# Folding the two key blocks of a windowed attention into one square of scores

## The reference

```
dist = arange(w)[:, None] + w - arange(2 * w)[None, :]
valid = (dist >= 0) & (dist < w) & (key_abs >= 0)
s = where(valid, s - slopes * dist, -inf)
m = maximum(max(s, axis=-1), sink)
p = exp(s - m)
p = p / (sum(p, axis=-1) + exp(sink - m))
o = einsum('bnhgqk,bnkhd->bnqhgd', p, vb)
return (o * silu(z)) @ w_out
```

## Time and profile before

| | |
|---|---|
| median of 3 runs | 1959.88 us (1953.9 to 1959.93) |
| profiled execution, its own time | 1960.14 us |
| its span | 1958.4 us |
| PE busy | 1878.6 us (96% of the span) |
| DVE busy | 1139.6 us (58%) |
| ACT busy | 717.4 us (37%) |
| layer 1's four groups | from about 1314 us to 1750 us of the span |

### The profile page before, as it was taken

The page is one execution under the profiler, slowest core; times in us unless marked ns, Lnnn a source line. Parts: engine busy times, 40 slices in busy tenths (PEclk is TensorE's granted clock), DMA queues, the critical chain, the costliest instruction groups (busy, mean ns, idle before and its releaser), DMA issues.

```text
span 1958.4 us, 30563 instructions
## 1 busy us (share of the span) xinstructions
PE 1878.6 (96%) x12644; PEld 1450.3 (74%) x12644; DVE 1139.6 (58%) x2143; ACT 717.4 (37%) x1517; POOL 6.4 (0%) x9
## 2 busy tenths in 40 slices
PE   6899999999999999999997899899999999999996
PEld 0267778778787877878775688777777777777885
DVE  2456574757557476665755666746656665663333
ACT  3343342424334252332524222524433443443221
POOL 0000000000000000000000000000000000000001
PEclk7999999999999999999998899999999999999998
DMA  9943233232332322232330777433323223313333
GB/s 392 409 169 136 97 116 117 97 136 97 109 123 104 121 106 104 100 132 97 130 109 1 254 244 236 158 135 118 114 97 130 103 108 123 130 54 113 135 108 118
DMA packets 59337, 268.24 MB, mean 137 GB/s; under 512 B 6584, under 2 KB 6968, under 8 KB 41664
## 3 DMA queue, kind: packets, MB, share of 16 engines
q1 hardware_dynamic: 59200, 266.30, 37.2%
HBM read 257.34 MB, written 8.93 MB: 136 GB/s over the span
## 4 chain that ended last, share of the span: by engine, by line
PE 86%; DVE 5%; ACT 4%; DMA 4%; issue 0%; SPq 0%; DVEq 0%; ACTq 0%
PE psum L576 25%; PE psum L577 23%; PE psum L578 23%; PE psum L699 2%; DMA ada_p<-in_ada_first 2%; PE psum L977 2%; DMA ada_t<-in_ada_first 1%; ACT pr L1346 1%; PE psum L989 1%; PE psum L1005 1%; PE psum L817 1%; DVE w_lo L1429 1%; PE psum L591 1%; PE psum L835 1%; DVE pr L1873 1%; DVE st L1880 1%
## 5 line engine op out<-in xcount | busy, mean ns | idle before, releaser
L576 PE MATMUL psum<-mov_hi,w_hi 128*128 128x512 f32 x2128 | 867.0, 407 | 28.9 <-DVE mov_lo L1471 9.0
L577 PE MATMUL psum<-mov_lo,w_hi 128*128 128x512 f32 x2128 | 834.2, 392 | 0.0
L578 PE MATMUL psum<-mov_hi,w_lo 128*128 128x512 f32 x2128 | 833.5, 392 | 0.0
L576 PEld LDWEIGHTS psum<-mov_hi,w_hi 128*128 128x128 f32 x2128 | 401.7, 189 | 156.7 <-issue 68.0
L578 PEld LDWEIGHTS psum<-mov_hi,w_lo 128*128 128x128 f32 x2128 | 402.0, 189 | 88.2
L577 PEld LDWEIGHTS psum<-mov_lo,w_hi 128*128 128x128 f32 x2128 | 403.0, 189 | 73.4
L1429 DVE TENSOR_TENSOR w_lo<-w_raw,w_hi 128x512 fp32r<-128x512 f32 x532 | 356.2, 687 | 172.5 <-ACT w_hi L1075 172.0
L1075 ACT ACTIVATE w_hi<-w_raw 128x512 fp32r<-128x512 f32 x532 | 310.6, 621 | 3.7 <-DMA w_raw<-in_w_pack 3.3
L1444 DVE SCALAR_TENSOR_TENSOR ada_acc<-ada_t,silu_c,ada_acc 128x512 f32<-128x512 f32 x240 | 179.3, 747 | 9.0 <-DVE ada_acc L1444 1.4
L1346 ACT ACTIVATE pr<-pr,st 128x256 f32<-128x256 f32 x128 | 63.5, 498 | 153.1 <-DVE st L1882 153.1
L1303 ACT ACTIVATE osq<-res 128x512 f32<-128x512 f32 x30 | 19.0, 633 | 234.3 <-DVE res L1828 234.3
(11 more groups left out here) (282 smaller groups left out, 1559.1 us busy)
## 6 DMA issues: line engine op xcount, KB each, us to landing
w_raw<-in_w_pack SPq DMA_DIRECT2D x133, 1024.0 KB, 4.8
ada_t<-in_ada_late SPq DMA_DIRECT2D x128, 512.0 KB, 5.7
x_in<-in_ada_first SPq DMA_DIRECT2D x32, 512.0 KB, 9.2
ada_t<-in_ada_first SPq DMA_DIRECT2D x16, 512.0 KB, 9.2
ada_p<-in_ada_first SPq DMA_DIRECT2D x16, 512.0 KB, 9.5
res<-in_x_t SPq DMA_DIRECT2D x4, 1024.0 KB, 11.5
xr<-in_x_t SPq DMA_DIRECT2D x16, 256.0 KB, 3.7
x_spill<-res SPq DMA_DIRECT2D x16, 256.0 KB, 5.4
```

What stands on the lines that cost most here:

```text
L576: mm(PJ[r], w_hi[r][:, ks], mov_hi[:, kt], start=(j == 0), stop=False)
L577: mm(PJ[r], w_hi[r][:, ks], mov_lo[:, kt], start=False, stop=False)
L578: ins = mm(PJ[r], w_lo[r][:, ks], mov_hi[:, kt], start=False, stop=(j == KC - 1))
```

## The change

Both triangles are put into one square. DVE writes slope * dist - score for both key blocks into a new tile `both`, and takes the minimum of the two blocks into `pr`, now 128 x 512 for a unit: where a score is invalid its value is about 1e30 times the slope, so the minimum picks the valid one. Minima, exponentials and division then run on 512 columns in place of 1024, and PE turns 4 blocks in place of 7, alternating between banks `TR` and `OA`. The copy of the turned blocks on ACT goes away; in its place DVE multiplies the turned square by a mask for either triangle, which gives the two halves of `prT` (`turn1_parts`), in the same slots 17 and 20. The masks are two more blocks of 128 columns in `dist1`. The value products stay.

```diff
-    second = np.concatenate([block0, band, band, band], axis=1).astype(np.float32)
+    second = np.concatenate([block0, band, band, band, p[:, None] > p[None, :], p[:, None] <= p[None, :]], axis=1).astype(np.float32)
...
+        both = [sb(f"both{i}", [P, T], where=l1) for i in range(2)]
+        pr = [sb(f"pr{i}", [P, T], where=l1) for i in range(2)]
...
             def turn1(g, u):
                 pe.wait_ge(r1_ok, g * GH + u + 1)
-                if u > 0 or g > 0:
-                    pe.wait_ge(ev1_ok, g * GH + u)
+                wait(pe, ev1_ok, g * GH + u - 1)
                 for n in range(4):
-                    for j in range(2):
-                        if n == 0 and j == 0:
-                            continue
-                        ins = nc.tensor.transpose(tr1(n)[:, j * P:j * P + P],
-                                                  pr[u % 2][:, n * 256 + j * P:n * 256 + j * P + P], ident)
+                    ins = nc.tensor.transpose((TR, OA)[u % 2][:, n * P:n * P + P], pr[u % 2][:, n * P:n * P + P], ident)
                 ins.then_inc(tr1_ok, 1)
...
             def exps1(g, u):
                 act.wait_ge(m1_ok, g * GH + u + 1)
                 for n in range(4):
-                    f(pr[u % 2][:, n * 256:n * 256 + 256], pr[u % 2][:, n * 256:n * 256 + 256], ACT.Exp,
+                    f(pr[u % 2][:, n * P:n * P + P], pr[u % 2][:, n * P:n * P + P], ACT.Exp,
...
-            def turn1_copy(g, u):
-                act.wait_ge(tr1_ok, g * GH + u + 1)
-                if u >= 2 or g > 0:
-                    act.wait_ge(pv1_ok, g * 4 + u // 2)
-                f(prT[u % 2][:, P:1024], psum[:, 4:6, :].rearrange("p a c -> p (a c)")[:, P:1024], ACT.Copy)\
-                    .then_inc(ev1_ok, 1)
...
             def biased1(g, w, hf):
 
                 dve.wait_ge(s1_ok, 8 * g + 2 * w + hf + 1)
+                for r in range(2):
+                    if g + w + hf > 0:
+                        dve.wait_ge(mn1_ok, 16 * g + 4 * w + 2 * hf - 1 + r)
+                    V.scalar_tensor_tensor(out=both[r][:], in0=dist1[:, hf * 512:hf * 512 + 512],
+                                           scalar=con("slope1")[:, g * GH + 2 * w + r:g * GH + 2 * w + r + 1],
+                                           in1=(SA0, SA1)[r], op0=ALU.mult, op1=ALU.subtract).then_inc(t1_ok, 1)
                 if hf == 0:
                     wait(dve, tr1_ok, GH * g + 2 * w)
                 for r in range(2):
-                    V.scalar_tensor_tensor(out=pr[r][:, hf * 512:hf * 512 + 512], in0=dist1[:, hf * 512:hf * 512 + 512],
-                                           scalar=con("slope1")[:, g * GH + 2 * w + r:g * GH + 2 * w + r + 1],
-                                           in1=(SA0, SA1)[r], op0=ALU.mult, op1=ALU.subtract).then_inc(t1_ok, 1)
+                    dve.wait_ge(t1_ok, 16 * g + 4 * w + 2 * hf + r + 1)
+                    two = both[r][:].rearrange("p (n j c) -> p n j c", n=2, j=2)
+                    V.tensor_tensor(pr[r][:, hf * 256:hf * 256 + 256].rearrange("p (n c) -> p n c", n=2),
+                                    two[:, :, 0, :], two[:, :, 1, :], ALU.min).then_inc(mn1_ok, 1)
+
+            def turn1_parts(g, u):
+
+                dve.wait_ge(tr1_ok, g * GH + u + 1)
+                if u >= 2 or g > 0:
+                    dve.wait_ge(pv1_ok, g * 4 + u // 2)
+                for j in range(2):
+                    part = dist1[:, 1024 + j * P:1024 + j * P + P].unsqueeze(1).to_broadcast([P, 4, P])
+                    ins = V.tensor_tensor(tile4(prT[u % 2][:, j * T:j * T + T]), tile4((TR, OA)[u % 2]), part, ALU.mult)
+                ins.then_inc(ev1_ok, 1)
...
+                    st.setdefault(L1_T[g][w][0], []).append(lambda w=w: turn1_parts(g, 2 * w))
+                    st.setdefault(L1_T[g][w][1], []).append(lambda w=w: turn1_parts(g, 2 * w + 1))
```

More of the change, by code:

```diff
@@ L183, in build @@
         l1 = ExitStack()
-        dist1 = sb("dist1", [P, 4 * 256], where=l1)
+        dist1 = sb("dist1", [P, 4 * 256 + 2 * P], where=l1)
         kcur = sb("kcur", [P, P + T], where=l1)
@@ L198, in build @@
         q1 = sb("q1", [P, 4 * T], where=l1)
-        pr = [sb(f"pr{i}", [P, 1024], where=l1) for i in range(2)]
+        both = [sb(f"both{i}", [P, T], where=l1) for i in range(2)]
+        pr = [sb(f"pr{i}", [P, T], where=l1) for i in range(2)]
         prT = [sb(f"prT{i}", [P, 1024], where=l1) for i in range(2)]
@@ L339, in build @@
         m1_ok = sem("m1_ok")
+        mn1_ok = sem("mn1_ok")
         p1_ok = sem("p1_ok")
@@ L964, in v_second @@
                 ins.then_inc(vup_ok, 1)
-            tr1 = lambda n: psum[:, 4 + n // 2, (n % 2) * 256:(n % 2) * 256 + 256]
             def scores1(g, w, hf):
@@ L1005, in values1 @@
                             ins = mm(GO[R[r], n * P:n * P + P], vcur[:, n - 1 + j, :],
-                                     prT[r][:, n * 256 + j * P:n * 256 + j * P + P],
+                                     prT[r][:, j * T + n * P:j * T + n * P + P],
                                      start=(j == 0 or n == 0), stop=(j == 1))
@@ L1361, in group_stages @@
                     st.setdefault(16 * w + 14, []).append(lambda w=w: exps1(g, 2 * w + 1))
-                    st.setdefault(L1_T[g][w][0], []).append(lambda w=w: turn1_copy(g, 2 * w))
-                    st.setdefault(L1_T[g][w][1], []).append(lambda w=w: turn1_copy(g, 2 * w + 1))
                 return st
@@ L1872, in biased1 @@
                 for r in range(2):
-                    V.scalar_tensor_tensor(out=pr[r][:, hf * 512:hf * 512 + 512], in0=dist1[:, hf * 512:hf * 512 + 512],
-                                           scalar=con("slope1")[:, g * GH + 2 * w + r:g * GH + 2 * w + r + 1],
-                                           in1=(SA0, SA1)[r], op0=ALU.mult, op1=ALU.subtract).then_inc(t1_ok, 1)
+                    dve.wait_ge(t1_ok, 16 * g + 4 * w + 2 * hf + r + 1)
[10 more added lines that the diff above has]
+                ins.then_inc(ev1_ok, 1)
             def maxima1(g, w, r):
                 u, s_ = g * GH + 2 * w + r, st1[r]
-                dve.wait_ge(t1_ok, 16 * g + 4 * w + 3 + r)
+                dve.wait_ge(mn1_ok, 16 * g + 4 * w + 3 + r)
                 step(V.tensor_reduce(s_[:, 0:4], blk(pr[r][:]), AX, ALU.min))
@@ L1889, in normalize1 @@
                 V.tensor_tensor(blk(pr[u % 2][:]), blk(pr[u % 2][:]),
-                                s_[:, 12:16].unsqueeze(2).to_broadcast([P, 4, 256]), ALU.mult).then_inc(r1_ok, 1)
+                                s_[:, 12:16].unsqueeze(2).to_broadcast([P, 4, P]), ALU.mult).then_inc(r1_ok, 1)
             def gated1(g, w):
```

## The result

The changed kernel takes **1939.63 us** (median of 4 runs, 1937.06 to 1943.35) against 1959.9 us (4 runs, 1953.9 to 1959.93). The ratio is 0.9909, 95% interval 0.9894 to 0.9924: 14.9 to 20.8 us less. The two profiled executions took 1960.14 and 1941.9 us, 18.2 apart. The prediction said 1942.1 us, 18.0 less. The two medians are 20.3 us apart here and 16.8 in the later series of run 8, so medians of so few runs can't be trusted to the microsecond.

A forecast was written before the change was run, and what follows sets the result against it. PE's instruction list was taken to bound the kernel, DVE and ACT counting only where PE waits. Savings of 10.5 + 6.8 + 0.65 = 18.0 us from 1960.1 gave 1942.1 us, range 1936 to 1950.

The forecast's parts named there:

- The transposes: PE's turns in layer 1: four transposes for seven, cost by count, 0.33 us a unit over 32 units, 10.5 us saved.
- The wait at slot 17: PE's wait for DVE's first division in 12 of 16 rounds goes, the chain being 0.8 us shorter: 6.8 us saved.
- DVE's added work: Layer 1: DVE takes on 2.3 us a round, reaches the gate 1.3 us later, hidden by its 3.7 us wait; cost 0.
- rival B: DVE's queue takes part of the gain back once products cost 1.3 us more each; 1950 us, chance 0.08.
- The end of the last group: PE's 3.61 us stop for the first `mov_lo` shrinks through a shorter chain from the last scores: 0.65 us saved.
- rival D: More than forecast: shorter stop at the group's end keeps the clock up, and a low run; 1936 to 1940, chance 0.09.
- a wait of PE for a low part: Sign that the prediction is wrong: PE waiting for a low part or for `prT` in layer 1.
- A: The wait at slot 17 stays because the chain is no shorter: 1949.6 us, halfway 1946; chance 0.15.
- C: DVE's time goes by instruction, not column, so the chain is 1.0 us longer: 1964.4 us; chance 0.05.
- The sum: Savings of 10.5, 6.8 and 0.65 us together: 18.0 us off the profiled 1960.1 us.

The follow-up runs named there:

- run 8: The changed kernel again, unaltered, on the chip of run 3, Run 6 and run 7: 1941.49 us, ratio 0.9914.
- run 1: The changed kernel with three of each unit's four transposes done twice, so seven again: 1951.66 us.
- run 2: The kernel before with the first unit's turn at slot 18 in place of 17, all work as it was: 1953.18 us, ratio 0.9978.
- run 3: The changed kernel with the row minima of each round's first unit done three times: 1958.23 us.
- run 4: The changed kernel with every masked product done once more into a scratch tile, 4 more products a round: 1942.53 us.
- run 5: The changed kernel with every masked product done three more times into a scratch tile, 12 more products a round: 2037.63 us, ratio 1.041.
- Run 6: The changed kernel with the output weights' second chunk's first low part ahead of two gated-result pieces on DVE at the last group's end: 1939.85 us.
- run 7: As Run 6, and on ACT the last high part stands ahead of the last unit's exponentials: 1937.75 us, ratio 0.9896.

## Why the prediction was right

**The transposes (10.5 us said).** Right: 0.44 us a turn, and run 1 shows that 90 transposes cost 10.3 us in the rounds. That the cost goes by count, without a fixed part, is shown by both.

**The wait at slot 17 (6.8 us said).** Right in size and cause. Run 2 removes it by a slot's delay and gains 6.6; run 3 brings it back by lengthening the chain. Reading only the idle column would have given 4.2; the difference of starts across the turn gave the right number. The reason given for the difference, the late weight load, is the smaller part of it: 0.07 us a turn beside 0.16 from the overlap of the rows (run 2). In the trace of after the first division ends 8.91 us after the start of the second scores (9.74 before), 0.83 less where 0.8 was said.

**DVE's added work (cost 0).** Right in effect, but by a wrong working, so in part by luck. I said that DVE would come to the gate 1.3 us later and its wait shrink by that much, to 2.4; it shrank by 0.5, to 3.2. In round 1 of the second group (second scores start at 1460.24 before, at 1454.85 after), first before, then after:

```profile
1477.42 0.69 DVE L1429 TENSOR_TENSOR w_lo<-w_raw,w_hi 128x512 fp32r<-128x512 f32 x1 [1.64 <-ACT w_hi L1075]
...
1484.49 0.69 DVE L1896 SCALAR_TENSOR_TENSOR res<-psum,res 128x512 f32<-128x512 f32 x1 [4.25 <-PE psum L1005]
```

```profile
1471.45 0.68 DVE L1415 TENSOR_TENSOR w_lo<-w_raw,w_hi 128x512 fp32r<-128x512 f32 x1
...
1477.91 0.69 DVE L1899 SCALAR_TENSOR_TENSOR res<-psum,res 128x512 f32<-128x512 f32 x1 [3.65 <-PE psum L1000]
```

Counted from the second scores, DVE comes to the gate at 20.0 us before and 19.4 after: 0.6 earlier, not 1.3 later. Its second division ends 1.26 us earlier, where 0.8 was said, and the 1.64 us for which it used to wait for a high part are filled with the products. That high part, which before stands on ACT behind the copy and its wait of 3.23 us for the transposes, ends 17.2 us after the second scores before and 12.0 after; had it come at 17.2 again, DVE, there at 16.6, would still have waited about 0.6. Against this, the working left out that PE comes to the values 1.2 us earlier (22.45 and 21.26 us), which shortens the wait.

The larger fault is that the gate's wait was taken for the cover. PE waits for the second product and not for the gate, and the margin there is 5.2 us in ordinary rounds and 2.7 in last ones (runs 4 and 5). So rival B's edge of 1.3 us a product was too low: run 4 comes to 1.4 and loses nothing, and by the margins that it left the edge is, as an estimate, 1.6 in a group's last rounds and 2.0 in ordinary ones. That the last rounds are the first to go was said rightly. Two numbers of that part were off as well: a round before took 28.6 us (429.5 in 15), not 27.5, and DVE's busy time rose by 24.3 us, not 36.

**The end of the last group (0.65 us said, beside two turns of 0.33).** The stop fell from 3.61 to 2.89 us, 0.72. The stretch shrank by 1.7, 0.4 more than the 1.3 said. Here something was missed. The granted clock stayed up behind the stop (starts 0.23 us apart instead of the 0.43 of the earlier trace rows), as rival D allowed, which should be worth 1.8 us; but a new stop of 1.74 us, where the one before was 0.38, took most of it: PE came sooner to a low part that DVE had not reached. Run 6 shows that by moving the low part. Run 4 shows the other side: its clock was down there, it had no second stop, and the stretch took 26.7 us all the same. So the near agreement of this term is partly luck, two things left out against each other; and a wait of PE for a low part, named as a sign of being wrong, did appear, though here alone and not in the rounds.

**The rivals.** A, that the wait stays, and C, that DVE's time goes by instruction, fell with the trace of after: no waiting turn, and minima of 419 ns beside products of 682. B is right as a mechanism, and begins only at an estimated 3.7 us of further DVE work a round. The sum, -18.0, stands against -18.2 between the two profiled executions; the rounds gave -17.0 where 30 turns and the wait had been put at -16.7.

## What to carry to other kernels

Where one engine's list is the time, an edit is worth the instructions it takes off that list, times their pitch, plus every wait whose chain it shortens; what it puts on another engine is free up to the time between the end of the result that the first one needs and the moment it needs it. That margin is read from two rows, in the round where it is smallest; the other engine's own waiting time, 3.2 us here against margins of 2.7 and 5.2, is not the margin. Once the margin is gone, the stops can cost more than their idle time, since the clock fell behind them (run 5). The cost of a wait is the difference from start to start across it, against a neighbour that doesn't wait: the idle column missed a third of it, mostly because rows overlap. When a stop gets shorter, look at what the engine reaches sooner, since here most of one gain turned into a wait for a low part 5 us later.

## What the runs showed of the hardware

A stop of one length can be followed by a fall of TensorE's clock in one execution and by none in another. After the output projection's first two chunks PE stops for 2.3 us in every trace, waiting for a low part of the weights. In the changed kernel's profiled execution the granted clock is down behind it, in that of run 7 it is not (busy time by stretch, columns as in the earlier trace rows):

```profile
1764.00:1775.00 11.00, 8.69 (x32) 6.76 (x31) 6.88 (x11) 6.87 (x12) 0.00 (x0) 0.84 0.68 239
```

```profile
1762.00:1773.00 11.00, 8.70 (x39) 6.89 (x38) 6.92 (x11) 6.87 (x12) 0.00 (x0) 1.00 0.68 240
```

In the same 11 us, with the same idle time, one has 32 products and the other 39. From the last value products to the last residual step it is 167.9 us in the first and 166.3 in the second, and the eight other traces, before and the experiments, give 166.3 or 166.4 (three) and 167.9 or 168.0 (five), whatever was edited. The like is seen at the stop before the output projection. The changed kernel, and then run 4, both with an idle time of 2.89 us there:

```profile
1735.00:1745.00 10.00, 5.37 (x25) 3.95 (x25) 8.34 (x16) 10.00 (x26) 0.00 (x0) 1.00 0.01 3
```

```profile
1735.00:1745.00 10.00, 7.18 (x25) 5.51 (x26) 8.70 (x16) 10.00 (x24) 0.00 (x0) 0.83 0.01 2
```

The first kept the full 2.4 GHz, the second fell to 1.2 GHz for part of it. What decides it was not tried. That this makes up part of the spread between executions of one kernel is likely but not shown: the two traces of the changed kernel agree, with 167.9 and 168.0.
